# A two-layer hybrid attention trunk on one core: rotated queries of branch B for four heads at a time, and a new order of small work in branches D and B

## What is computed

```
h = split_cols(x @ w_in)
A: softmax(q k^T * scale + decay differences) v          causal, dense
B: c_q, c_kv = rms_norm(...)                             ranks 256 and 128
   q = c_q @ w_uq: per head 64 plain columns, then 32 that are rotated
   k, v = c_kv @ w_ukv; k gets one rotated 32-column key shared by all heads
   rope(x): [x1*cos - x2*sin, x1*sin + x2*cos], x1 and x2 the halves of the 32
C: attention over the 256 keys that an indexer picks (top-k)
D: window of 128 keys, with a sink in the softmax's sum
y = concat(A, B, C, D, each times silu(gate)) @ w_out
x = layer_norm(ALPHA * x + y)
```

## Time and profile before

| | |
|---|---|
| median of 3 runs | 3026.89 us (3025.06 to 3029.12) |
| the profiled execution's own time | 3021.65 us |
| its span in the trace | 3019.8 us |
| PE busy | 2882.5 us, 95% |
| DVE busy | 1654.9 us, 55% |
| ACT busy | 1065.7 us, 35% |
| POOL busy | 642.5 us, 21% |
| mean granted TensorE clock | 0.992 |
| layer 1: D / B, us from the span's start | 532 to 804 / 804 to 1066 |

### The profile page before, as it was taken

How to read it: one execution, slowest core, us unless ns; L and a number is a source line. 1 busy time by engine, 2 the same in 40 slices (tenths; PEclk the granted TensorE clock), 3 DMA queues, 4 the chain that set the end, 5 groups by cost and what they waited for, 6 DMA issues and landing times. The chain is left out here.

```text
span 3019.8 us, 39749 instructions
## 1 busy us (share of the span) xinstructions
PE 2882.5 (95%) x13686; PEld 1689.7 (56%) x13686; DVE 1654.9 (55%) x4445; ACT 1065.7 (35%) x3129; POOL 642.5 (21%) x1336
## 2 busy tenths in 40 slices
PE   7999999998899999999999999999988999999998
PEld 5446666555466666644544466665544666666443
DVE  5338887666777433322233388877667774333232
ACT  3233444333445444510012334443334453445000
POOL 1002333111122244410000023321111222445000
PEclk9999999999999999999999999999999999999999
DMA  5101111101000011142120011111010000210421
GB/s 214 62 10 44 43 43 32 45 25 48 15 22 19 22 61 73 30 141 84 56 89 29 15 39 43 43 39 38 27 46 22 17 19 23 106 32 27 155 84 42
DMA packets 89101, 152.65 MB, mean 51 GB/s; under 512 B 10640, under 2 KB 66592, under 8 KB 86856
## 3 DMA queue, kind: packets, MB, share of 16 engines
q1 hardware_dynamic: 88904, 150.12, 15.1%
HBM read 120.12 MB, written 32.08 MB: 50 GB/s over the span
## 5 line engine op out<-in xcount | busy, mean ns | idle before, releaser
L1096 PE MATMUL ps_s<-xT,w_ring 128*128 128x348 f32 (+4 forms) x3616 | 1126.4, 465 | 14.8 <-DVE gate L1552 6.6
L1096 PEld LDWEIGHTS ps_s<-xT,w_ring 128*128 128x128 f32 x3616 | 673.6, 191 | 408.7 <-issue 115.5
L1347 ACT ACTIVATE arena<-ps_t 16x32 f32<-16x32 f32 (+4 forms) x1104 | 371.6, 364 | 248.5 <-PE ps_t L1166 231.8
L1334 ACT ACTIVATE arena<-arena,small 128x1040 f32<-128x1040 f32 (+8 forms) x544 | 372.7, 685 | 144.8 <-DVE small L1614 144.4
L1377 DVE MAX8 small<-score 128x8 f32<-128x1040 f32 (+6 forms) x448 | 376.4, 840 | 10.5
L1379 DVE MATCH_REPLACE8 score<-small,score 128x1040 f32<-128x1040 f32 (+6 forms) x448 | 370.0, 826 | 0.0
L1166 PE MATMUL ps_t<-ident,arena 128*128 128x128 f32 (+1 forms) x2016 | 296.7, 277 | 9.9 <-ACT arena L1347 9.8
L1726 POOL TENSOR_SCALAR strips<-arena,small 128x16 f32<-128x16 f32 x384 | 107.1, 279 | 927.2 <-DVE small L1626 927.2
L1166 PEld LDWEIGHTS ps_t<-ident,arena 128*128 128x128 f32 (+1 forms) x2016 | 229.4, 140 | 124.1 <-issue 70.2
L1139 PE MATMUL ps_s<-feat 64*128 64x272 f32 (+12 forms) x1680 | 296.2, 455 | 0.0
L1729 POOL TENSOR_SCALAR arena<-arena,small 128x1024 f32<-128x1024 f32 (+7 forms) x384 | 286.2, 745 | 0.0
(11 more groups left out here) (168 smaller groups left out, 2504.7 us busy)
## 6 DMA issues: line engine op xcount, KB each, us to landing
w_ring<-in_w_feat SPq DMA_DIRECT2D x78, 512.0 KB, 3.5
mixed<-mixg SPq DMA_DIRECT2D x128, 128.0 KB, 1.7
feat<-mixed SPq DMA_DIRECT2D x16, 1024.0 KB, 6.5
resid<-score SPq DMA_DIRECT2D x16, 512.0 KB, 3.1
score<-resid SPq DMA_DIRECT2D x16, 512.0 KB, 7.3
arena<-in_w_out SPq DMA_DIRECT2D x4, 1536.0 KB, 8.1
cT<-falls SPq DMA_DIRECT2D x8, 520.0 KB, 4.8
feat<-falls SPq DMA_DIRECT2D x8, 520.0 KB, 5.4
```

The source lines that it names most:

```text
L1096: mm = pe.matmul(ps_s[:, bank, 0:w], w_ring[:, wt % 2, k, :], xT[:, k, c0:c0 + w], start=(k == 0), stop=(k == KT - 1))
L1334: nc.scalar.activation(p, p, ACT.Exp, scale=-1.0, bias=nm[:, e:e + 1], accum_out=psums[0:M, st % 4, e:e + 1]).then_inc(S["exp_done"], 1)
L1347: a = nc.scalar.activation(dst, src, ACT.Copy)
```

## The change

Five things, all in the order of work around D and B:

1. **Rotated queries.** `q_rope` makes R products for a group of four heads (128 rows, no swapped copy), ACT copies them out. The two halves of each head are then swapped by eight DMAs between SBUF tiles (`sw`), DVE rotates the whole tile in three operations of 1,040 columns (`rot`, steps 0 to 2), and two more DMAs make a second copy with its 64-row halves exchanged (`dup`), from which the other pair and the other row group read. Group 0 stands in D's fourth pair, group 1 in B's first and second. `cos_t` and `sin_t` take the place of `rope_t`.
2. **D's transposes** come as one group of four.
3. **D's fillers** all stand behind that group (`between = 0`).
4. **B's values** go through the free score banks, two at a time, and so does TB of the 16-row block, which moves one step ahead. The `ct` of that block and of block 7 trade places.
5. **Waits.** A pair's first step waits only for projections that it reads (`ready`), not for all so far.

```diff
     if br == "D":
-        return [both(i), both(i - 1)] if e else []
+        return [[(h, kb) for h in range(2) for kb in (i - 1, i)]] if e else []
...
     def q_latent(self, l, p):
-        return [lambda c=c, what=what: self.add("qb", l=l, p=p, what=what, cols=asked(l)[c],
-                                                **self.group("act" if what == "N" else "dve", P_BANK))
-                for what in "RN" for c in range(3)]
+        return [lambda c=c: self.add("qb", l=l, p=p, what="N", cols=asked(l)[c], ct_end=self.ct_end,
+                                     **self.group("act", P_BANK, scored=True)) for c in range(3)]
+
+    def q_rope(self, l, g, c, bank=P_BANK):
+
+        it = self.add("qb", l=l, p=g, what="R", cols=asked(l)[c], ct_end=self.ct_end, **self.group("act", bank))
+        self.rope_end = it["nth"]
...
                 for idx, b in zip((6, 7, 8), range(3 * p, 3 * p + 3)):
-                    put(idx, lambda b=b: self.token_block(l, "TB", b))
+                    if b == NB - 2:
+                        put(idx, lambda: self.token_block(l, "TB", NB - 1, bank=self.free_bank()))
+                    if b < NB - 1:
+                        put(idx, lambda b=b: self.token_block(l, "TB", b))
                     if b:
-                        put(idx, lambda b=b: self.latent(l, b - 1))
+                        put(idx, lambda b=b: self.latent(l, b if b == NB - 1 else b - 1))
+                if p == NP - 2:
+                    put(8, lambda: self.add("uw", l=l))
             else:
-                put(1, lambda: self.latent(l, NB - 1))
-                put(0, lambda: self.add("uw", l=l))
-                work = [lambda b=b: self.token_block(l, "VB", b) for b in range(NB)]
-                for idx, fn in zip((3, 3, 4, 4, 5, 5, 6, 6, 7, 4, 5, 6, 7, 8, 8), work + self.q_latent(l, 0)):
-                    put(idx, fn)
+                put(0, lambda: self.latent(l, NB - 2))
+                for idx in (1, 2):
+                    fill[idx].insert(0, lambda c=idx - 1: self.q_rope(l, 0, c, bank=self.free_bank()))
+                put(4, lambda: self.turn(l, 0, "sw"))
+                for b in range(NB):
+                    idx = 3 + b // 2
+                    if b < NB - 1:
+                        put(idx, lambda b=b: self.token_block(l, "VB", b, bank=self.free_bank(b % 2)))
+                    else:
+                        put(idx, lambda b=b: self.token_block(l, "VB", b))
+                    if b == 1:
+                        put(idx, lambda: self.q_rope(l, 0, 2))
+                for idx, work in zip((4, 5, 6), self.q_latent(l, 0)):
+                    put(idx, work)
+                for idx, step in ((5, 0), (6, 1), (6, 2), (7, "dup")):
+                    put(idx, lambda step=step: self.turn(l, 0, step))
                 early = lambda: self.k_latent(l, 0)
         elif br == "B":
             if p + 1 < NP:
-                for idx, work in zip((3, 4, 5, 6, 7, 7), self.q_latent(l, p + 1)):
+                for idx, work in zip((3, 4, 5), self.q_latent(l, p + 1)):
                     put(idx, work)
+                if p == 0:
+                    for c in range(3):
+                        put(6 + c, lambda c=c: self.q_rope(l, 1, c))
+                elif p == 1:
+                    for idx, step in ((0, "sw"), (2, 0), (3, 1), (4, 2), (5, "dup")):
+                        put(idx, lambda step=step: self.turn(l, 1, step))
...
+                elif kind == "sw":
+                    g, c0 = it["g"], asked(l)[0][0]
+                    sp.wait_ge(S["pj_act"], it["nth"])
+                    half = ROPE // 2
+                    for r in range(0, BLK, half):
+                        sp.dma_start(qr_t[g][1][r:r + half, c0:NTOK], qr_t[g][0][r ^ half:(r ^ half) + half, c0:NTOK]
+                                     ).then_inc(S["swap_ld"], 16)
+                elif kind == "dup":
+                    g, c0 = it["g"], asked(l)[0][0]
+                    sp.wait_ge(S["rot_done"], 2 * l + g + 1)
+                    for e in range(2):
+                        sp.dma_start(qr_t[g][1][HD * e:HD * e + HD, c0:NTOK],
+                                     qr_t[g][0][HD * (1 - e):HD * (1 - e) + HD, c0:NTOK]).then_inc(S["two_ld"], 16)
...
+                    if it["idx"] == 0 and br == "B" and p % 2 == 0:
+                        pe.wait_ge(S["two_ld"], 32 * (2 * l + p // 2 + 1))
...
+                elif kind == "rot":
+                    g, step, c0 = it["g"], it["step"], asked(l)[0][0]
+                    raw, swapped = [t[:, c0:NTOK] for t in qr_t[g]]
+                    if step == 0:
+                        dve.wait_ge(S["swap_ld"], 128 * (2 * l + g + 1))
+                        link(dve.tensor_tensor(swapped, swapped, sin_t[:, c0:NTOK], ALU.mult))
+                    elif step == 1:
+                        link(dve.tensor_tensor(raw, raw, cos_t[:, c0:NTOK], ALU.mult))
+                    else:
+                        dve.tensor_tensor(raw, raw, swapped, ALU.add).then_inc(S["rot_done"], 1)
```

More of the change, by code:

```diff
@@ L204, in __init__ @@
         self.bank_owner = [None] * 7
+        self.ready = dict(pj_act=0, pj_dve=0)
+        self.cn_of, self.ct_end, self.rope_end = {}, 0, 0
         self.row_owner = [None] * 3
@@ L248, in next_slot, with group @@
         return 2 - 2 * self.slot
-    def group(self, by, bank):
+    def group(self, by, bank, scored=False):
         g, k = self.take("pj"), self.take("pj_" + by)
+        if scored:
+            self.ready["pj_" + by] = k + 1
         return dict(g=g, bank=bank, free=self.banks([bank], ("pj_" + by, k + 1)), nth=k + 1)
@@ L267, in token_block @@
     def token_block(self, l, what, b, bank=P_BANK):
-        cn = self.take("cn") if what == "TB" else None
+        cn = self.cn_of[(l, b)] = self.take("cn") if what == "TB" else None
         by = "dve" if (what, b) in (("TC", 0), ("TA", NB - 1)) else "act"
-        self.add("tm", l=l, what=what, b=b, cn=cn, xt=self.xt_of[(l, b)], **self.group(by, bank))
+        self.add("tm", l=l, what=what, b=b, cn=cn, xt=self.xt_of[(l, b)], ct_end=self.ct_end, **self.group(by, bank))
     def y_half(self, l, b, yy, half):
@@ L281, in latent @@
     def latent(self, l, b):
-        self.add("ct", l=l, b=b, cn=NB * l + b, tg=self.take("tg"))
+        self.add("ct", l=l, b=b, cn=self.cn_of[(l, b)], tg=self.take("tg"))
+        self.ct_end = self.n["tg"]
     def open(self):
@@ L292, in chunk @@
         self.add("mt", l=l, what=what, wt=wt, cols=pieces[c], last=self.left[wt] == 0, gin=gin,
-                 **self.group("dve" if what in ("G", "IK") else "act", bank), **kw)
+                 **self.group("dve" if what in ("G", "IK") else "act", bank, scored=what != "G"), **kw)
     def tile(self, l, what, **kw):
@@ L311, in k_latent @@
         for c, bank in enumerate((free, P_BANK, 2 - free)):
-            self.add("kb", l=l, p=p, cols=CHUNKS[c], **self.group("act", bank))
+            self.add("kb", l=l, p=p, cols=CHUNKS[c], **self.group("act", bank, scored=True))
     def layer(self, l):
@@ L380, in index @@
                 self.row_owner[row] = ("acc_done", acc + 2)
-                self.add("ix", l=l, p=p, i=i, n=n, chunks=chunks, acc=acc, row=row, rwaits=rwaits)
+                self.add("ix", l=l, p=p, i=i, n=n, chunks=chunks, acc=acc, row=row, rwaits=rwaits,
+                         ready=sorted(self.ready.items()) if i == NB - 1 else [])
                 if p == 0 and i == 3:
@@ L478, in pair @@
             work = fill.get(idx, [])
-            for fn in work[:1]:
+            between = 0 if br == "D" else 1
+            for fn in work[:between]:
                 fn()
@@ L482, in pair @@
             self.add("exp", e=1, **s)
-            for fn in work[1:]:
+            for fn in work[between:]:
                 fn()
@@ L1114, in _ @@
                     i = it["i"]
-                    if i == NB - 1:
-                        waits(pe, [(n, it["upto"][n]) for n in ("pj_act", "pj_dve")])
+                    waits(pe, it["ready"])
                     iq = iq_t[it["p"] % 2]
```

85 lines of the change are left out of this document (42 added, 43 removed).

## The result

The changed kernel runs in 2944.56 us (median of 4 runs, 2943.56 to 2945.63) against 3026.89: ratio 0.9727, 95% interval 0.9715 to 0.9739. That is 82.3 us less; 64.5 were forecast, 2962.4, and 2944.56 lies at the range's lower edge. The profiled execution took 2943.56 us, its span is 2941.6.

What follows compares the result with a forecast made beforehand. PE, busy 95% of the span, and its 137 us of idle time were taken as the bound. Terms -14.0 - 67.0 - 2.6 + 6.8 + 3.0 + 4.8 + 4.5 = -64.5 us gave 2962.4 us on the median, range 2944 to 2988.

Steps and rivals of the forecast that it cites:

- What bounds: Whole kernel: PE works 95% of the span, so time is PE's work plus its 137 us of idle time.
- R products, -14.0, and clock, -2.6: 12 fewer R products at 1.17 us save 14.0 us; slow clock after B's 2.60 us wait goes, 1.3 a layer.
- Waits removed, -67.0: PE's waits at `ct`, B's values and query products, 67.0 us together, all counted as gone.
- The two late `ct`, +6.8 and +3.0: PE waits for DVE's scaling: 3.4 us a layer at the 16-row block's `ct`, 1.5 at block 7's.
- Last pair and chain, +4.8: D's last pair: 0.45 us twice a layer for ACT's copies, plus 1.5 a layer for the rotation chain.
- 2 us to spare: D's fourth pair: last swap lands 6 us after `sw`, DVE's first rotation comes at 8 us.
- Bare steps, +4.5: B's second and third pairs lose fillers in steps 6 to 8; transposes wait 1.13 us a pair for ACT.
- One group, narrower waits and table at nothing: D's single group, the narrower `ready` waits and the added 520 KB table at the start: no cost.
- Swaps in series: Rival: swaps land one after another, DVE stands 9.6 us in D's last pair; +20, 2982 us; chance 0.14.
- The waits only move: Rival: P_BANK, transposes' banks and top-k bind in more of D's steps; +24, 2986 us; chance 0.13.
- Better than forecast: Rival: 3.4 us waits shrink, their slow stretch goes, B's bare steps cost little; about 2945 us; chance 0.11.
- slower than before: Rival: B's first scores stand on the chain, swaps at 6.5 us each; near 3035 us; chance 0.04.

Runs made afterwards that it cites:

- d_groups: Changed kernel with D's transposes in two groups again and its first filler between them: 2973.06 us, ratio 0.9822.
- values_pbank: Changed kernel with all nine of B's values through P_BANK again: 2965.49 us, ratio 0.9795.
- cs_ahead: Changed kernel with DVE scaling the last two latent blocks ahead of top-k work and the gate's operation: 2933.61 us, ratio 0.9692.
- pair_rope_free: Changed kernel with rotated queries again made per pair and rotated by DVE, two R chunks in D through a free score bank: 2963.57 us, ratio 0.9790.
- ready_all: Changed kernel with a pair's first step waiting again for all projections so far: 2954.24 us, ratio 0.9769.
- spread_357: Changed kernel plus the edits of cs_ahead and top_light, last two query products moved to steps 6 and 8 in B and C pairs: 2918.71 us, ratio 0.9646.
- top_light: Changed kernel with three top-k operations moved out of the two-rotation step of D's fourth pair: 2934.90 us, ratio 0.9700.
- ct_places: Changed kernel with the last two `ct` and the 16-row block's TB back in their old places: 2951.69 us, ratio 0.9748.

## Why the prediction was right, and where it was off

- **What bounds.** Right: PE, and the waits of the earlier trace rows. Its idle time fell by 50.1 us, in D and B by 47.4 against a forecast of 47.9. That the two agree so closely is partly luck: in D an error of 4.6 us met others of about the same size the other way, both below.
- **R products, -14.0, and clock, -2.6.** 144 records instead of 192, as said. B's busy time fell by 18.6 instead of 16.6: by 14.8 in its second and third pairs, where the twelve products stood and no slow stretch fell (1.24 us each instead of 1.17), and by 3.8 in its first pair, where both layers lost a slow stretch and the waits with it. The product's price was a little low: 1.17 us is one in a row of others, while the ones removed stood partly behind waits (next section).
- **Waits removed, -67.0.** Right. The run d_groups shows that the single group with the fillers behind it freed `ct` (which of the two, no run tells), values_pbank that the banks freed the values.
- **The two late `ct`, +6.8 and +3.0.** Right to 0.1 us each, and by the cause given: cs_ahead moved DVE's scaling, and of 3.4 and 1.6 us a layer 0.8 to 1.0 and nothing were left. Both were of the change's own making, and the cheapest thing left to mend.
- **Last pair and chain, +4.8.** Mis-sized. The scores behind two values wait 0.75 + 0.60 and, in layer 2, 1.8 us a layer for a forecast of 0.9. The chain was put at 1.5 us a layer; the value product waits 3.05 and 3.16, of which 0.8 and 0.9 stay when the chain is gone (pair_rope_free), so 2.2 to 2.3 are its own. In all 9.4 us stand where 4.8 were forecast. The step that failed is "push DVE about 2 us behind PE in the short steps": the 2 us were right, but I let them end at B's first scores, while DVE's lateness passed on through ACT's queue to a copy that PE needed a step sooner. It made no difference to the sum of idle time, because other waits in D shrank for which I had counted nothing: 0.6 us in layer 1 and 2.1 in layer 2 at TB, gate and value products by PE's timeline, 0.6 a layer at B's first scores (1.3 us in the row of before), and some 0.4 a layer in gaps too short for a row. The swaps' "2 us to spare" was wrong too: their issues took 5.03 us instead of 3.7 and DVE came 7.2 us after the first instead of 8, so 0.4 us were to spare in layer 1 and 0.2 lacked in layer 2. It cost almost nothing.
- **Bare steps, +4.5.** Right: 0.77 at the transposes of each of the four pairs and 0.2 to 0.6 at a value product in three of them, 4.2 in all. B's first pairs kept 1.2 us for which nothing was forecast.
- **One group, narrower waits and table at nothing.** Wrong for the waits. They are worth 3.0 us against the kernel before (3.9 for issue at the indexer, less 0.9 more for ACT there), and ready_all shows 4.7 more that the new order would have had without them.
- **Busy time unpriced, 7.8 us in D and B.** The sum had PE's busy time fall by the work removed and two slow stretches alone. It fell by 5.9 in D with the same instructions and without help from the clock: by the traces' clock records D spent 17.0 us at 1.2 GHz before and 20.4 after. What fell is the number of waits, from 50 to 15 in the two layers' D (next section).
- **Outside D and B, 6.4 us.** Of it 2.7 are idle, the 1.5 a layer at the indexer above less small waits that grew. Of the 3.7 of busy time 3.0 are in the first row and are clock: the start lost its slow stretches (0.99 to 1.00).
- **The rivals.** Swaps in series would have cost 22 us, 20 were forecast; they aren't in series. "The waits only move" is refuted by 87.2 us of idle time, though in small it is what the value product, the scores and the indexer show. "Better than forecast" had the right time for the wrong reasons: neither of its waits shrank, and bare steps cost what was said; the 11.5 us of busy time brought it there. The 3035 of "slower than before" doesn't follow from its own terms: 42 us from `sw` are the break-even, and eight swaps of 6.5 us are 52, ten more in each layer, so 3047.

## What the runs showed of the chip

**A wait costs more than its length.** Groups by line on PE, before and then after: TB products, query products, values.

```profile
L1066 PE MATMUL ps_s<-vw,xT 128*128 128x512 f32 x256 | 115.8, 606 | 1.4 <-ACT squares L1260 1.4
...
L1105 PE MATMUL ps_s<-cT,vw 128*128 128x348 f32 (+3 forms) x192 | 66.6, 470 | 17.6 <-DVE feat L1570 8.0 <-ACT arena L1251 5.6 <-ACT feat L1311 3.5
...
L1059 PE MATMUL ps_s<-vw,cT 128*128 128x512 f32 (+1 forms) x36 | 19.6, 627 | 13.9 <-DVE feat L1570 7.3 <-ACT arena L1251 6.3
```

```profile
L1130 PE MATMUL ps_s<-vw,xT 128*128 128x512 f32 x256 | 113.0, 594 | 1.6 <-ACT squares L1324 1.6
...
L1170 PE MATMUL ps_s<-cT,vw 128*128 128x348 f32 (+3 forms) x144 | 47.9, 455 | 0.0
...
L1123 PE MATMUL ps_s<-vw,cT 128*128 128x512 f32 (+1 forms) x36 | 17.1, 593 | 0.0
```

The same instruction is shorter: 594 for 606 ns, 455 for 470, 593 for 627. Without a wait a group starts some 0.15 us before the one ahead of it ends (in the timeline of the changed kernel, transposes from 747.42 for 0.66, values from 747.92; the ends of such records are modelled by the profiler); with a wait that overlap is lost and counted mostly as busy time. The lengths of whole pairs don't hang on modelled ends. In d_groups D's first two pairs of both layers, none with a slow stretch, have 13 more waits than in the changed kernel, 17.9 us in sum, and are 19.8 us longer: 0.14 us more for each wait, from 0.07 to 0.30 by pair. The order of transposes and fillers differs too between the two kernels, and what share that has isn't shown. The Trainium skill (TensorE: Matmul & The Clock Gate, Step-by-step: what each phase is for) says that the drain of one product overlaps the fill of the next; the trace agrees as far as the records' overlap goes, and so a wait removed is worth its length and, by this estimate, about 0.14 us more. For the 35 waits fewer in D that is some 5 us, near the 5.9 by which D's busy time fell; the rest isn't accounted for. Part of the shorter means is clock, which these rows don't separate.

**Slow stretches of the clock.** PE runs for short stretches at 1.2 instead of 2.4 GHz, in every kernel here, and where one falls a pair is 1.5 us longer with the same instructions and waits: C's third pair in layer 1 takes 60.68 us in the changed kernel, 59.18 in the one before. They come with waits of about 3 us in D (both 3.4 us waits had one; layer 2's at 3.16 us had one, layer 1's at 3.05 had none), but also where the longest wait near is under 1 us, as in C's bare step:

```profile
1198.00:1206.00 8.00, 6.80 (x46) 4.19 (x46) 1.77 (x15) 4.86 (x23) 4.38 (x12) 0.79 0.06 19
```

In spread_357, whose steps in B and C are filled and whose waits in D are gone, none is left in D, B or C. What makes one begin isn't settled: top_light took a 3 us wait away in layer 1 and got a stretch some steps earlier. No single edit's gain should be read closer than about 3 us here, and that is also why ct_places and top_light can't be told from the changed kernel by time alone.

## What to carry to other kernels

When small transposes stand behind groups of others and need the other engine's copy of one of them, keep to one group and put a long product between; that was worth 29 us here, 25 of them idle time. Products that take turns in one bank gain from banks of their own: 21 us, 12.5 of them idle time. When a step hands work to an engine that also feeds the critical one, look one step further than the consumer: the two rotations were in time for their reader and still cost over 2 us a layer, through the maxima queued behind them. And look in each queue for small operations that stand behind divisible work, as the scaling did behind top-k: moving them ahead gave 11 us, 7 of them idle time and the rest mostly clock.
